# Modulation columns of the opening computed directly, the weight chunk as stationary operand

## The reference

```python
mod_ctx = modulation(c_ctx, w_ada[l], b_ada[l])[None, None, :]     # silu(c_ctx) @ w_ada + b_ada, 6144 values
mod_lat = modulation(c, w_ada[l], b_ada[l])[:, None, :]
...
shift1, scale1, gate1, shift2, scale2, gate2 = jnp.split(mod, 6, axis=-1)
h = rmsnorm(x, norm1_g) * (1.0 + scale1) + shift1
proj = h @ w_in
```

## Time and profile before

| what | value |
|---|---|
| median of 3 runs | 1280.67 us (1279.39 to 1280.92) |
| the profiled execution | 1278.3 us |
| its span, first to last instruction | 1276.6 us |
| PE busy in the span | 1238.8 us (97%) |
| PE's share of the chain that ended last | 79% |
| L1155, the rows of the modulation | 96 records, 23.2 us busy |

### The profile page before, as it was taken

How to read it: one execution, slowest core, us unless ns; L and a number is a source line. 1 busy time by engine, 2 the same in 40 slices (tenths; PEclk the granted TensorE clock), 3 DMA queues, 4 the chain that set the end, 5 groups by cost and what they waited for, 6 DMA issues and landing times.

```text
span 1276.6 us, 19504 instructions
## 1 busy us (share of the span) xinstructions
PE 1238.8 (97%) x7590; PEld 1130.9 (89%) x7590; DVE 902.9 (71%) x1437; ACT 519.3 (41%) x893; POOL 398.5 (31%) x295
## 2 busy tenths in 40 slices
PE   4999999999999999999999999999999999999997
PEld 2698888899999999987888898899998999889985
DVE  4658787368456899853999754488964799548966
ACT  5442222464133444324777422364431344214434
POOL 1012210220564545201899200015500454006400
PEclk9999999999999999999999999999999999999999
DMA  9644664133322354560200216212232223322222
GB/s 309 218 132 140 206 219 137 33 108 106 110 67 81 102 157 125 148 215 11 74 1 1 83 66 215 66 34 66 69 130 67 67 67 100 99 66 67 91 91 83
DMA packets 89721, 134.91 MB, mean 106 GB/s; under 512 B 3673, under 2 KB 64594, under 8 KB 89378
## 3 DMA queue, kind: packets, MB, share of 16 engines
q1 hardware_dynamic: 77024, 95.69, 23.4%
q0 software_dynamic: 8144, 30.11, 7.2%
q10 hardware_dynamic: 4466, 7.92, 2.4%
HBM read 120.06 MB, written 7.36 MB: 100 GB/s over the span
## 4 chain that ended last, share of the span: by engine, by line
PE 79%; DVE 9%; POOL 6%; ACT 3%; issue 1%; DMA 1%; ACTq 0%; DVEq 0%
PE psum L514 29%; PE psum L746 24%; PE psum L461 18%; POOL probs L1114 4%; POOL probs L1120 3%; DVE seven_lo L776 2%; PE psum L447 1%; PE psum L664 1%; DVE w_lo L430 1%; PE psum L1155 1%; PE psum L1263 1%; DMA rows<-in_diff_subln_g 1%; PE psum L1248 1%; PE psum L1261 1%; PE psum L1262 1%
## 5 line engine op out<-in xcount | busy, mean ns | idle before, releaser
L430 DVE TENSOR_TENSOR w_lo<-w_raw,w_hi 128x2048 fp32r<-128x2048 f32 x45 | 106.6, 2370 | 104.1 <-ACT w_hi L425 101.7
L766 ACT ACTIVATE seven_hi<-w_raw 128x512 fp32r<-128x512 f32 x160 | 99.5, 629 | 154.5 <-PE psum L746 101.9
L776 DVE TENSOR_TENSOR seven_lo<-w_raw,seven_hi 128x512 fp32r<-128x512 f32 x160 | 140.9, 911 | 20.8 <-ACT seven_hi L766 20.6
L746 PE MATMUL psum<-h_hi,seven_lo 128*128 128x320 f32 x464 | 143.6, 310 | 1.1 <-DVE silu_g L2277 1.1
L746 PE MATMUL psum<-h_hi,seven_hi 128*128 128x320 f32 x464 | 143.6, 309 | 0.0
L746 PE MATMUL psum<-h_lo,seven_hi 128*128 128x320 f32 x464 | 143.6, 309 | 0.0
L425 ACT ACTIVATE w_hi<-w_raw 128x2048 fp32r<-128x2048 f32 x45 | 85.9, 1910 | 132.3 <-PE psum L514 87.6
L514 PE MATMUL psum<-w_hi,hid 128*128 128x512 f32 x440 | 135.6, 390 | 0.0
L514 PEld LDWEIGHTS psum<-w_hi,hid 128*128 128x128 f32 x440 | 82.7, 188 | 16.9
L514 PE MATMUL psum<-w_lo,h_hi 128*128 128x512 f32 x240 | 95.0, 396 | 0.3 <-DVE w_lo L430 0.3
L514 PE MATMUL psum<-w_hi,h_hi 128*128 128x512 f32 x240 | 93.6, 390 | 0.0
(11 more groups left out here) (354 smaller groups left out, 3267.1 us busy)
## 6 DMA issues: line engine op xcount, KB each, us to landing
w_raw<-in_w_in SPq DMA_DIRECT2D x32, 1024.0 KB, 6.3
chain_b<-in_w_ada POOLq DMA_DIRECT2D x24, 512.0 KB, 4.5
w_raw<-in_w_ffn_gate SPq DMA_DIRECT2D x11, 1024.0 KB, 5.4
w_raw<-in_w_ffn_up SPq DMA_DIRECT2D x11, 1024.0 KB, 5.3
ada_a<-in_w_ada SPq DMA_DIRECT2D x8, 1024.0 KB, 13.6
w_raw<-in_w_ffn_down SPq DMA_DIRECT2D x8, 1024.0 KB, 5.0
ada_b<-in_w_ada POOLq DMA_DIRECT2D x8, 512.0 KB, 4.2
w_raw<-in_w_ret_out SPq DMA_DIRECT2D x4, 1024.0 KB, 5.1
```

Source lines behind the costliest of these rows:

```text
L430: dve.tensor_tensor(w_lo[s][:, :, :], w_raw[s][:, :, :], w_hi[s][:, :, :].bitcast(F32), ALU.subtract).then_inc(w_lo_done, 1)
L746: last = pe.matmul(banks[p], w[:, p, k, :], x[:, k, :], start=(k == 0 and m == 0), stop=(k == KH - 1 and m == 2))
L766: done = act.activation(seven_hi[:, p, :, :], of_weights(p, name, i, par), ACT.Copy)
L776: done = dve.tensor_tensor(seven_lo[:, p, :, :], of_weights(p, name, i, par), seven_hi[:, p, :, :].bitcast(F32), ALU.subtract)
```

## The change

The six chunks that went through PE as rows now have the chunk as stationary operand: for each half m of the chunk (128 channels) and each k-tile the 128x128 piece of `w_ada` is loaded into the array, and the two silu values for each row pass it, 2 columns. The result of 8 such matmuls is a 128x2 tile, which is the columns wanted. A chunk so takes 16 matmuls with 2 columns (32 records) where there were 8 with 256 columns (16 records) and two transposes. ACT's six copies, `mod_rows` and the waits on `ada_row` go. The columns of odd pairs move from PSUM bank 7 to bank 6. SP's refill of two buffers waits for `ada_used`, raised at the end of the first two of the new blocks. The groups of products of k = 2 and k = 3, which a row stood between, now follow each other.

```diff
         def shift_or_scale(pair, kind):
-            return bank(7, 4, 8 * pair + 4 * kind)
+            return bank(6 + pair % 2, 4, 8 * pair + 4 * kind)
...
             for n in range(2):
-                sp.wait_ge(ada_row_ps, n + 1)
+                sp.wait_ge(ada_used, n + 1)
                 load_first_ada(n, 3, n)
...
-            def ada_row_of(n, buf, use):
-                if n:
-                    pe.wait_ge(ada_row, n)
+            def ada_columns(pair, kind, buf, use):
+                if pair >= 2:
+                    pe.wait_ge(q["scale"], pair - 1)
                 pe.wait_ge(ada_a_in[buf], 16 * use)
-                for k in range(KT):
-                    last = pe.matmul(psum[0:2, 6 * BANK:6 * BANK + UC], silu_c[:, k, :], ada_a[buf][:, k, :],
-                                     start=(k == 0), stop=(k == KT - 1))
-                last.then_inc(ada_row_ps, 1)
-            def ada_columns(n, pair, kind):
-                pe.wait_ge(ada_row, n + 1)
-                if pair:
-                    pe.wait_ge(q["scale"], pair)
                 for m in range(2):
-                    last = pe.transpose(shift_or_scale(pair, kind)[:, 2 * m:2 * m + 2], mod_rows[0:2, n % 3, m * P:(m + 1) * P],
-                                        ident[0:2, 0:2])
+                    for k in range(KT):
+                        last = pe.matmul(shift_or_scale(pair, kind)[:, 2 * m:2 * m + 2], ada_a[buf][:, k, m * P:(m + 1) * P],
+                                         silu_c[:, k, :], start=(k == 0), stop=(k == KT - 1))
                 return last
...
-            ada_row_of(0, 0, 1)
+            ada_columns(0, 0, 0, 1).then_inc(ada_used, 1)
...
-            ada_columns(0, 0, 0)
-            ada_row_of(1, 1, 1)
+            ada_columns(1, 0, 1, 1).then_inc(ada_used, 1)
...
-            ada_row_of(2, 2, 1)
-            ada_columns(1, 1, 0)
-            ada_columns(2, 1, 1).then_inc(ada_cols, 1)
+            ada_columns(1, 1, 2, 1).then_inc(ada_cols, 1)
...
-            ada_row_of(3, 3, 1)
-            pe.wait_ge(q["lo"], 3)
-            first_products(2, three)
-            ada_row_of(4, 0, 2)
-            ada_columns(3, 2, 0)
+            ada_columns(2, 0, 3, 1)
+            for k in (2, 3):
+                pe.wait_ge(q["lo"], k + 1)
+                first_products(k, three)
             pe.wait_ge(ada_pre, 32)
             sums_over_partitions(pe, 1, shift_or_scale(2, 1), ada_acc0).then_inc(ada_cols, 1)
-            ada_row_of(5, 1, 2)
-            ada_columns(4, 3, 0)
-            pe.wait_ge(q["lo"], 4)
-            first_products(3, three)
-            ada_columns(5, 3, 1).then_inc(ada_cols, 1)
+            ada_columns(3, 0, 0, 2)
+            ada_columns(3, 1, 1, 2).then_inc(ada_cols, 1)
...
-            def evacuate_row(n):
-                act.wait_ge(ada_row_ps, n + 1)
-                act.activation(mod_rows[:, n % 3, :], psum[0:2, 6 * BANK:6 * BANK + UC], ACT.Copy).then_inc(ada_row, 1)
```

More of the change, by code:

```diff
@@ L202, in build @@
         x_T = at("x_T", H + 20, [P, KT, TOK])
-        mod_rows = at("mod_rows", A + 37, [2, 3, UC])
         o_nat = at("o_nat", H, [P, TILES, D])
@@ L367, in build @@
         sub_ready = sem("sub_ready")
-        ada_row_ps, ada_row, ada_cols = sem("ada_row_ps"), sem("ada_row"), sem("ada_cols")
+        ada_used, ada_cols = sem("ada_used"), sem("ada_cols")
         x_scaled = sem("x_scaled")
@@ L1482, in _ @@
                 act.activation(x_nat[:, t, :], x_nat[:, t, :], ACT.Copy, scale=rstd[:, t:t + 1]).then_inc(x_scaled, 1)
-            def evacuate_row(n):
-                act.wait_ge(ada_row_ps, n + 1)
-                act.activation(mod_rows[:, n % 3, :], psum[0:2, 6 * BANK:6 * BANK + UC], ACT.Copy).then_inc(ada_row, 1)
-            evacuate_row(0)
             for k in range(KT):
@@ L1494, in _ @@
             act.activation(w_hi[0][:, :, :], w_raw[0][:, :, :], ACT.Copy).then_inc(w_hi_done, 1)
-            evacuate_row(1)
             def modulate_pair(p):
@@ L1511, in _ @@
             act_split(act, 1, 1)
-            evacuate_row(2)
             act.wait_ge(kc_ps, 1)
@@ L1515, in _ @@
             modulate_pair(1)
-            for n in (3, 4):
-                evacuate_row(n)
             modulate_pair(2)
-            evacuate_row(5)
             modulate_pair(3)
```

## The result

The changed kernel takes 1292.25 us, the median of 6 runs (1291.15 to 1293.33), against 1280.76 us of before in the same job (6 runs, 1278.38 to 1281.04). The ratio is 1.0094, 95% interval 1.0083 to 1.0104: slower by 0.9%. The forecast, 1278.8 us, was wrong in sign, and the time lies 2 us above the range. The profiled execution took 1291.8 us, 13.5 above that of before.

A forecast was written before the change was run, and what follows sets the result against it. PE, busy 97% of the span, was taken to bound the kernel. Savings of 1.26 before the first product, 0.45 on later blocks and 0.19 on joined groups made -1.9 us: 1278.8 us from 1280.67, range 1276.5 to 1290.

The forecast's parts named there:

- the whole sum of -1.9 us: Opening, up to the long piece: -1.26 before the first product, -0.45 for three later blocks, -0.19 for joined product groups.
- a block at 3.6 us: Each new group of 32 records on PE: 0.112 us a record, 3.6 us against the old 3.75.
- 36 records of products at 5.47: Groups of first products in the opening: 36 joined records take 5.47 us, against 5.66 for two groups of 18.
- the first product: After the transposes of x: products can start at 35.96 us, 1.26 us earlier than before.
- the long piece: 312 records of products in one piece closing the opening: would begin near 58.8 us in place of 60.7.
- the second unit's low part in time: Second weight unit's split on DVE ends at 39.02 us, unmoved; PE needs it at 39.6, cover 0.6 us.
- the translation to the median of before: From profile to timed runs: profiled 1276.4 us, plus 2.4 us between profile and earlier median, gives 1278.8 us.
- The step on block 0: First new block, from 16.7 us: cost 0 if the clock rises at the same point; otherwise 7.2 us, 1.7 too late.
- The clock rival: Opening: 2-column blocks fail to raise or keep PE's clock; 1285.4 us, ends 1281.8 and 1299, chance 0.32.
- The stall: New blocks: sums into the same column wait for each other, 7.8 us a block, 1300 us; chance 0.02.
- the dear block: New blocks cost 3.92 us each, so the gain does not arrive, 1280.4 us; within the no-change rival, chance 0.12.
- the lost covers: Margins of 0.2, 0.6 and 1 us at h, second weight unit, pair 3; two lost means no change, chance 0.12.

The follow-up runs named there:

- warm start: The wide kernel plus five unread matmuls of ident, 256 columns each, in PE's idle time before the first new block; 1276.64 us, ratio 0.9971.
- the wide kernel: The changed kernel with 128 columns instead of 2 passing in all 96 new matmuls, the silu values repeated 64 times; 1275.95 us, ratio 0.9967.

## Why the prediction was wrong

**The step that failed** is the one under the whole sum of -1.9 us: every term of it is priced at the full clock, a block at 3.6 us, block 0 at a cost of 0 and 36 records of products at 5.47, and the case in which the clock falls was put at a chance of 0.32. In the runs the clock was down in block 0 and fell three times more in the opening, and that cost 16.0 us. The sum for a clock that holds is right. With 128 columns its terms are: a block 3.57 us (forecast 3.6), the first product at 35.84 in PE's timeline (35.96; that kernel's transposes of x started 0.3 us later than before's), the long piece at 58.36 (58.8), no wait of PE in between, the second unit's low part in time. These terms are those of the run with 128 columns and the warm start; over the three profiles with 128 columns in every block the end of the opening lies 1.9 to 2.5 us below that of before's first profile, forecast 1.9. What was off beside it is the translation to the median of before: it added the 2.4 us between that median and the profile, and the wide kernel's median, 1275.95, has no such distance from its own profiled executions (1276.47 and 1275.86).

**The step on block 0** said "Cost 0, if the pace comes up at the same point". It did not; block 0 took 6.96 us, as the bound of 7.2 had it, and the transposes of x ran behind it at 6.71 for 4.68. The first block then was on the path: the chain starts with its DMA and holds no ACT.

**The clock rival** was the right mechanism at 0.32, and its price was too small, 6.6 us for a measured 16.0 (120.14 in the changed kernel, 104.12 in the wide one with warm start). By terms, from the two chains: the opening up to block 1, 3.5 us (forecast 0 for its middle, 6.4 at the end of its bounds); the blocks, 3.05 for block 2 and 2.9 for blocks 4 and 5 (forecast 3.6); the ones sums and the keys' transposes 0.6; the products, 2.7 and 1.6 for the groups of 36 and 1.9 in the long piece (forecast 3, for two places; there were three, since the clock fell behind block 3 alone too); less 0.2 because blocks 1 and 3 with 2 columns are a little cheaper at full clock, 3.47 for 3.57. Two of its questions are settled: a weight load of 128 columns in float32 runs at half pace at the lower level (0.217 us a record for 0.108), and the fall may come behind the block, in instructions that let 128 or 320 columns pass.

**The evidence was misread in weight.** The 4.6 us of transposes that kept the clock have 128 columns for each load; the longest group with few columns was 1.68 us, less than half a block. The prediction said that the rows can't exclude the fall, and still gave the case without it the larger chance. A change that takes a 256-column stream out of the engine and puts 2-column matmuls in went outside all that the trace had shown, and the range's upper end, 1290, was set below the rival's own bound of 1299.

The Trainium skill, TensorE: Matmul & The Clock Gate, Part 1 says that activity releases the throttle and its lack returns it. The traces agree in direction, and show that weight loads back to back with 2 columns each, an engine without a gap, neither raised the clock (6.96 us for block 0) nor kept it. Part 4 says that transposes don't count as activity in the same way; here the clock came up while PE did nothing but the transposes of x (10 records in 24 to 26 us, 18 in 28 to 30), so on this kernel they did.

**The stall, the dear block, the lost covers**: the changed kernel shows none of them; its blocks at full clock took 3.47 us. In the first trace of the wide kernel one cover did fail: the second weight unit landed at 35.7 us, its low part was ready only at 40.0, where the prediction had a fixed 39.02, and PE idled 0.63 us before the second half of the first products.

## What to carry to other kernels

Turning a product round so that the short side streams left PE busy and, at the full clock, the price of a chunk about as it was (3.47 us for 3.75), and it still halved the clock in part of the opening. Before such a change, compare the columns that pass in each stretch with the leanest stretch of the trace that kept the clock, and price the fall for everything behind it too. Where the weight load sets the pace anyway, more columns can cost next to nothing: here 128 for 2 cost 0.1 us a block, and reading the same values again with a step of zero was worth 16 us. Only 2 and 128 columns were run, so what lies between is not known. A busy share of 100% hides a clock at half; count records in windows of equal length.

## What the runs showed of the hardware

- A float32 matmul record with 128 loaded columns took 0.108 us from start to start with 2 columns passing and 0.112 with 128 (3.47 and 3.57 us for 32).
- At the lower clock the same record took 0.217 us (6.96 for 32). The weight loads themselves, timed as PEld, took 3.65 us for the 32 of block 1 and 6.95 for the 32 of block 2.
- A run of such records with 2 columns made the granted clock fall to 0.50 within blocks or up to 1.3 us behind them, in all six kernels with such blocks, with PE busy throughout; with 128 columns it fell in none of three profiles before PE stopped.
- The column of the granted clock says 1.00 until its first record, at 28.5 us of the changed kernel: at 24 to 26 us it read 1.00, with 10 transposes where 18 to 21 small records stand at full pace.
